# Gathering two expert rows per turn instead of four through a ring of eight places, with a quarter of the query weights kept in SBUF

## The chip, the cores and the metric

The kernel runs on one core of one Trainium2 chip. The metric is the device time of one launch in microseconds. The engines are TensorE (PE; its weight loads are listed apart as PEld), VectorE (DVE), ScalarE (ACT), GpSimd (POOL) and SyncE (SP); SP and POOL issue the transfers, which 16 DMA engines carry out.

## The reference

Two layers over 256 tokens of width 1024, everything in float32. Each layer has a mixer (four groups of heads, one output projection) and then an expert retrieval, which is where most of the bytes are:

```python
def peer(h, wq, keys, u_tab, v_tab):
    ...
        q = (xc @ wq).reshape(c, PEER_HEADS, 2, PEER_QDIM // 2)        # wq: 1024 x 2048
        sc = jnp.einsum('thpd,hpkd->thpk', q, keys, ...)
        top_v, top_i = lax.top_k(sc, PEER_TOPK)                         # 16 of 128, twice a head
        cand = (top_v[:, :, 0, :, None] + top_v[:, :, 1, None, :]).reshape(c, PEER_HEADS, -1)
        ...
        best_v, best_pos = lax.top_k(cand, PEER_TOPK)
        ids = jnp.take_along_axis(cand_id, best_pos, axis=-1)
        gate = jax.nn.softmax(best_v, axis=-1)
        ug = u_tab[ids]                                                 # 8 x 16 rows of 1024 for each token
        act = jax.nn.gelu(jnp.einsum('td,thkd->thk', xc, ug, ...)) * gate
        vg = v_tab[ids]
        return jnp.einsum('thk,thkd->td', act.astype(vg.dtype), vg)
```

Each token has 128 experts (8 heads, 16 each) of its own, and each expert is a row of u and a row of v, 4 KB each.

## The kernel before

The 256 tokens are two blocks of 128, one token to a partition. A pass n (0 to 3) is one block of one layer: passes 0 and 1 are layer 0, passes 2 and 3 are layer 1. In a pass, a slot is one of the 128 experts of all 128 tokens of the block. One indirect transfer of POOL (L1817) gathers u and v rows of one slot, 1 MB, into a place of `ring`, which has `RING` = 10 places. 512 slots go through it in all.

A turn takes `RING_G` = 4 slots. DVE makes the dot product of each u row with the block's normalised tokens as soon as the place has landed (L1354, "dots"). When the turn's four dots are there, ACT applies gelu (L839) and DVE multiplies by the gates (L1363, "weigh"). ACT then writes a diagonal matrix for each slot (L862), and PE adds diag x v to the PSUM sums in banks 0 and 1 (L1756, "rows of v"): four MATMUL records for each slot. When PE is through with a slot, `v_used` rises, and POOL gathers the next slot into that place. In turns 20 to 30 of passes 0 to 2, DVE adds the v row of the turn's fourth slot itself (L1370). The last two turns of all go slot by slot (L1377, L1384, L852, L1767).

The mixer and the expert search of the next pass are computed between turns. `plan_steps` writes one list of steps, and each engine walks it in order and does its part of each step; no scheduler changes it. In the turns 0 to 25 of a pass, the steps of the next pass stand between "weigh" and "rows of v": in turn 18 the transposes of its normalised rows ("rows 1", L1430), in turns 19 to 23 its query products ("query 0" to "query 3", L1720, each 1024 x 512 weights), scores (L1740) and searches ("best", "pairs", "ids", all on DVE).

Query weights are four quarters of 2 MB per layer (`wq_quarters`, `wq_at`). Quarter 0 stays in W for both passes of a layer. Quarters 1 to 3 are loaded by SP in each pass: in pass 0 partly into ring places that are not in use yet (quarter 1 into places 8 and 9, quarter 2 into 0 and 1), in pass 2 in 12 pieces of 512 KB, in passes 1 and 3 as L630, L631 and, when query 1 is through, L633. The first gathers wait for those ring places: gathers 6 and 7 for query 1 and gathers 8 and 9 for query 2 (`t in (6, 8)`).

## Time and profile before

| | |
|---|---|
| three runs, median (lowest to highest) | 1575.87 us (1573.58 to 1576.57) |
| the profiled execution, its time | 1571.93 us |
| its span, first to last instruction | 1570.1 us |
| PE, DVE, ACT, POOL busy | 1353.3, 1155.8, 454.2, 607.5 us |
| bytes moved | 627.87 MB, 400 GB/s on average |
| mean granted clock of TensorE | 0.957 |

The profiled execution lies 1.83 us above its span and 3.94 us below the median of the three runs. A windows view gives, for each stretch, the busy time of each engine, then the granted clock of PE, the mean share of the 16 DMA engines that were busy (1.01 is full) and the rate. "Idle before" is the time an engine stood still just before a group or an instruction, with what ended it.

### The profile page before, as it was taken

What the parts mean: (1) busy time and instruction counts of PE and PEld (TensorE: products, weight loads), DVE (VectorE), ACT (ScalarE), POOL (GpSimd) and SP (SyncE); (2) the same over time, 40 slices, a digit from 0 to 9 for tenths busy, and PEclk for the clock granted to TensorE, in tenths of its full rate; (3) what the DMA queues carried; (4) which work ended last, traced back from release to release, by engine and by line L of the source; (5) the groups of instructions that cost most, each with busy time, mean ns of one, the idle gap of its engine ahead of it and who ended that gap; (6) DMA issues with size and microseconds to landing.
All of it is one profiled execution on the core that took longest, in us unless ns stands there. A gap on an engine that the chain in (4) does not pass through costs nothing.

```text
span 1570.1 us, 15089 instructions
## 1 busy us (share of the span) xinstructions
PE 1353.3 (86%) x4622; PEld 735.0 (47%) x4622; DVE 1155.8 (74%) x2745; ACT 454.2 (29%) x1095; POOL 607.5 (39%) x525
## 2 busy tenths in 40 slices
PE   8899999998795997888897799999869777878777
PEld 4667455553472444453375345555337433333333
DVE  6937999787697886874578888985658987665545
ACT  3523154352211333342122134333212221121112
POOL 1012455444333334453433333644433443333331
PEclk9999999999898998999999899999979999999999
DMA  9558999999999999999999999999999999999997
GB/s 359 220 207 350 421 419 422 398 421 421 420 394 421 422 407 418 421 419 423 421 418 418 418 410 413 418 380 401 422 423 392 415 411 420 423 421 421 422 421 326
DMA packets 89820, 627.87 MB, mean 400 GB/s; under 512 B 10081, under 2 KB 11361, under 8 KB 20750
## 3 DMA queue, kind: packets, MB, share of 16 engines
q0 software_dynamic: 74144, 537.97, 83.2%
q1 hardware_dynamic: 15598, 88.95, 14.0%
q8 instruction: 38, 0.62, 0.2%
q14 instruction: 40, 0.33, 0.1%
HBM read 625.82 MB, written 1.06 MB: 399 GB/s over the span
## 4 chain that ended last, share of the span: by engine, by line
PE 41%; DMA 33%; DVE 16%; issue 6%; ACT 3%; POOL 1%; SPq 0%; POOLq 0%; DVEq 0%; ACTq 0%
DMA ring<-table_uv,ids 31%; PE ps L1756 24%; DVE ring L1354 6%; PE ps L1720 5%; PE ps L1520 4%; PE ps L1687 2%; PE ps L1510 1%; DMA ring<-w_in 1%; ACT acts L839 1%; ACT diag L862 1%; PE ps L1471 1%; PE ps L1587 1%; DVE weights L1363 1%; PE ps L1493 1%; POOL ring L1817 1%
## 5 line engine op out<-in xcount | busy, mean ns | idle before, releaser
L1756 PE MATMUL ps<-ring,diag 128*128 128x512 f32 x1884 | 877.3, 620 | 193.2 <-ACT diag L862 186.1
L1817 POOL DMA_INDIRECT ring<-table_uv,ids x512 | 601.9, 1175 | 927.0 <-PE ps L1756 780.1
L1756 PEld LDWEIGHTS ps<-ring,diag 128*128 128x128 f32 x1884 | 365.8, 199 | 654.6 <-issue 643.9
L1354 DVE CUSTOM_DVE_ANT_0 ring<-ring,h 128x1024 f32<-128x1024 f32 x384 | 456.3, 1224 | 155.5 <-DMA ring<-table_uv,ids 152.8
L839 ACT ACTIVATE acts<-dots,small 128x4 f32<-128x4 f32 x126 | 37.5, 297 | 875.5 <-DVE dots L1354 849.6
L1354 DVE CUSTOM_DVE_ANT_0 ring<-ring,ps 128x1024 f32<-128x1024 f32 x120 | 144.7, 1220 | 98.1 <-DMA ring<-table_uv,ids 97.9
L862 ACT ACTIVATE diag<-cst,weights 128x128 f32<-128x128 f32 x471 | 151.3, 390 | 28.9 <-DVE weights L1363 28.9
L1720 PEld LDWEIGHTS ps<-hT,W 128*128 128x128 f32 x896 | 101.9, 192 | 3.7 <-issue 2.9
L1720 PE MATMUL ps<-hT,W 128*128 128x128 f32 x896 | 103.1, 276 | 0.2 <-ACT hT L708 0.2
L1520 PE MATMUL ps<-W,hT 128*128 128x512 f32 (+2 forms) x160 | 60.1, 530 | 1.3 <-DVE hT L985 1.3
L1363 DVE TENSOR_TENSOR weights<-acts,gates 128x4 f32<-128x4 f32 x126 | 20.5, 163 | 51.4 <-ACT acts L839 51.4
L1687 PE MATMUL ps<-W,hT 128*128 128x512 f32 x128 | 57.3, 593 | 0.8 <-DVE hT L1199 0.8
L839 ACT ACT_TABLE_LOAD x43 | 55.2, 1283 | 2.2 <-DVE dots L1354 1.5
L1520 PEld LDWEIGHTS ps<-W,hT 128*128 128x128 f32 x160 | 30.4, 190 | 33.0 <-issue 30.6
L1370 DVE SCALAR_TENSOR_TENSOR x<-ring,weights,x 128x1024 f32<-128x1024 f32 x33 | 42.4, 1285 | 1.2
L1354 DVE DVE_READ_ACCUMULATOR2_ANT dots<- 128x1 f32 x504 | 41.4, 82 | 0.0
L1687 PEld LDWEIGHTS ps<-W,hT 128*128 128x128 f32 x128 | 24.0, 190 | 29.2 <-issue 28.2
L1510 PE MATMUL ps<-W,hT 128*128 128x512 f32 (+2 forms) x96 | 35.3, 523 | 1.3 <-DVE hT L985 1.3
L1587 PE MATMUL ps<-W 128*128 128x256 f32 (+1 forms) x128 | 32.0, 332 | 3.6 <-DVE h L1166 2.3
L770 ACT ACTIVATE W<-ps,small 128x128 f32<-128x128 f32 (+1 forms) x64 | 26.0, 418 | 12.3 <-DVE small L1135 12.2
L1134 DVE TENSOR_REDUCE small<-ps 128x4 f32<-128x512 f32 (+1 forms) x16 | 15.2, 953 | 17.7 <-PE ps L1594 10.2
L1510 PEld LDWEIGHTS ps<-W,hT 128*128 128x128 f32 x96 | 18.2, 190 | 19.4 <-issue 17.2
(319 smaller groups left out, 1201.1 us busy)
## 6 DMA issues: line engine op xcount, KB each, us to landing
W<-peer_wq SPq DMA_DIRECT2D x9, 2048.0 KB, 12.8
W<-w_out SPq DMA_DIRECT2D x6, 2048.0 KB, 12.5
W<-w_in SPq DMA_DIRECT2D x8, 1282.0 KB, 11.3
ring<-table_uv,ids POOLq DMA_INDIRECT x512, 13.4
W<-w_in SPq DMA_DIRECT2D x8, 898.0 KB, 10.0
W<-peer_wq SPq DMA_DIRECT2D x12, 512.0 KB, 13.1
W<-w_in SPq DMA_DIRECT2D x8, 768.0 KB, 9.8
W<-w_in SPq DMA_DIRECT2D x8, 514.0 KB, 11.8
```

The costliest lines, as they stand in the source:

```text
L839: a.activation(acts[:, g * RING_G:(g + 1) * RING_G], dots[:, g * RING_G:(g + 1) * RING_G], ACT.Gelu_apprx_tanh, scale=ffn_rstd[n % NB]).th ...
L862: a.activation(diag[:, s, :], ident, ACT.Copy, scale=weights[:, s:s + 1]).then_inc(diag_ready, 1)
L1354: v.tensor_tensor_reduce(ring_u[:, r, :], ring_u[:, r, :], tokens, 1.0, 0.0, ALU.mult, ALU.add, dots[:, s:s + 1]).then_inc(dots_done, 1)
L1363: v.tensor_tensor(weights[:, ss], acts[:, ss], gates[:, b, i * RING_G:(i + 1) * RING_G], ALU.mult)\
L1370: v.scalar_tensor_tensor(out=x[:, b, :], in0=ring_v[:, r, :], scalar=weights[:, s:s + 1], in1=x[:, b, :], op0=ALU.mult, op1=ALU.add).then_ ...
L1510: mm = pe.matmul(ps[:, 2 + i, 0:c1 - c0], hT[:, k, :], win_at(n)[:, k % 2, c0:c1], start=(k == 0), stop=(k == KC - 1))
L1520: mm = pe.matmul(ps[:, z_bank(n, i), 0:c1 - c0], hT[:, k, :], win_at(n)[:, slot, c0:c1], start=(k == 0), stop=(k == KC - 1))
L1587: pe.matmul(dst, q, k, start=True, stop=False)
L1687: mm = pe.matmul(ps[:, 2 + c, :], hT[:, k, :], half[:, k % 4, c * 512:(c + 1) * 512], start=(k == 0), stop=(k == KC - 1))
L1720: mm = pe.matmul(ps[:, 6 + q % 2, i * P:(i + 1) * P], src[:, k, :], hT[:, k, :], start=(k == 0), stop=(k == KC - 1))
L1756: mm = pe.matmul(ps[:, c, :], diag[:, s, :], ring_v[:, r, c * 512:(c + 1) * 512], start=(k == 0), stop=(k == SLOTS - 1), skip_group_check= ...
L1817: gp.indirect_dma_start(ring[:, place(t), :], None, table_uv, bass.IndirectOffsetOnAxis(ap=ids[:, b, k:k + 1], axis=0)).then_inc(pair_in[p ...
```

## The change

It does five things.

- A turn has two slots (`RING_G` = 2), so a pass has 64 turns instead of 32. The buffers for dots, weights and diagonals still hold 8 slots, which are now four turns (`BACK` = 4) instead of two.
- The ring has 8 places. In the room of the two others stands `wq_kept`: quarter 2 of the query weights is loaded once a layer and stays for its second pass. Passes 1 and 3 load quarters 1 and 3 only, both at once; pass 2 loads them in 8 pieces, and quarter 2 earlier. In pass 0, quarter 1 lies in places 0 and 1 (gathers 6 and 7 wait for query 1), and gather 8 onward waits for the release of gather 0 onward.
- The steps between turns: the list of each old turn is cut in the middle, first half in the first of its two new turns. A list of one step, and all of turn 0, goes to the second. In pass 0 the first searches are placed by a table (`first_search`), and ACT's copies of query 2 and 3 by steps of their own ("queried").
- The last slot of all: DVE adds its v row to the PSUM sums by two SCALAR_TENSOR_TENSOR of 512 columns (L1408 after the change) in place of diagonal, product and sum. The tokens x are added to PSUM by PE half way through pass 3.
- Behind two exponentials in pass 0, ACT does a small gelu, so that its table is loaded early.

```diff
-RING_G = 4
-HELD = 2 * RING_G
-RING = 10
-PLACES = (7, 2, 3, 4, 5, 6, 8, 9, 0, 1)
+RING_G = 2
+HELD = 8
+BACK = HELD // RING_G
+RING = 8
+PLACES = (7, 2, 3, 4, 5, 6, 0, 1)
+QUAD = 4 // RING_G
+TURNS = HALVES // QUAD
-SINGLE = HALVES * PASSES - 2
+SINGLE = HALVES * PASSES - HELD // RING_G
...
+    first_search = {2: ["best 1"], 4: ["best 2"], 5: ["best 3"], 6: ["pairs 1"], 7: ["ids 1"], 9: ["pairs 2"], 11: ["ids 2"]}
...
+            turn, part = i // QUAD, i % QUAD
+            turn_steps = [(name, n) for name in (own[turn] if n and turn < len(own) else [])]
+            turn_steps += [(name, n + 1) for name in (mixing[turn] if turn < len(mixing) else [])]
...
+            cut = len(turn_steps) // 2 if turn else 0
+            turn_steps = turn_steps[cut:] if part else turn_steps[:cut]
...
+        wq_kept = sb("wq_kept", [P, 4096])
...
-        wq_early = [by_key(t) for t in (pool[:, 16384:20480], pool[:, 0:4096], W[:, 2560:6656])]
+        wq_early = [by_key(t) for t in (pool[:, 0:4096], W[:, 2560:6656])]
...
-                sp.dma_start(wq_at(n, 1), wq_quarters[1]).then_inc(wq_in[1], 16)
-                sp.dma_start(wq_at(n, 2), wq_quarters[2]).then_inc(wq_in[0], 16)
-                sp.wait_ge(qT_ps, 4 * n + 2)
+                sp.dma_start(wq_at(n, 1), wq_quarters[1]).then_inc(wq_in[0], 16)
                 sp.dma_start(wq_at(n, 3), wq_quarters[3]).then_inc(wq_in[1], 16)
...
-                    v.wait_ge(low_done, 1)
-                    v.tensor_tensor(x[:, b, 0:512], x[:, b, 0:512], ps[:, 0, :], ALU.add).then_inc(x_low, 1)
-                    v.wait_ge(v_used, by_pe(HALVES * (n + 1)))
-                    v.tensor_tensor(x[:, b, 512:D], x[:, b, 512:D], ps[:, 1, :], ALU.add).then_inc(x_done, 1)
+                    v.wait_ge(weights_done, parts_done(m - 1) + k % RING_G + 1)
+                    v.wait_ge(v_used, by_pe(HALVES * (n + 1)) - 1)
+                    for c, done in ((0, x_low), (1, x_done)):
+                        v.scalar_tensor_tensor(out=x[:, b, c * 512:(c + 1) * 512], in0=ring_v[:, r, c * 512:(c + 1) * 512],
+                                               scalar=weights[:, sl:sl + 1], in1=ps[:, c, :], op0=ALU.mult, op1=ALU.add).then_inc(done, 1)
...
-                        elif t in (6, 8):
-                            gp.wait_ge(qT_ps, t // 2 - 1)
+                        elif t == 6:
+                            gp.wait_ge(qT_ps, 2)
```

PE's order at the first gathers of pass 0, before. L1720 is a query product, L1740 scores, L1756 rows of v, L1430 the transposes for pass 1, L1520 the projection of pass 1 (the input weights are W).

```order
L1740 MATMUL ps<-key_rows,zkv 128x128 x4
L1720 MATMUL ps<-hT,ring 128x128 x32
L1756 MATMUL ps<-ring,diag 128x512 x8
L1740 MATMUL ps<-key_rows,h 128x128 x4
L1720 MATMUL ps<-hT,W 128x128 x32
L1740 MATMUL ps<-key_rows,zkv 128x128 x4
L1430 MATMUL ps<-cst,x 128x128 x8
L1756 MATMUL ps<-ring,diag 128x512 x8
L1520 MATMUL ps<-W,hT 128x512 x3
```

The same place after the change (L1734 query, L1754 scores, L1770 rows of v, L1447 transposes, L1537 projection):

```order
L1754 MATMUL ps<-key_rows,zkv 128x128 x4
L1734 MATMUL ps<-hT,wq_kept 128x128 x32
L1770 MATMUL ps<-ring,diag 128x512 x8
L1754 MATMUL ps<-key_rows,h 128x128 x4
L1734 MATMUL ps<-hT,W 128x128 x32
L1770 MATMUL ps<-ring,diag 128x512 x4
L1447 MATMUL ps<-cst,x 128x128 x8
L1770 MATMUL ps<-ring,diag 128x512 x4
L1754 MATMUL ps<-key_rows,zkv 128x128 x4
L1770 MATMUL ps<-ring,diag 128x512 x4
L1537 MATMUL ps<-W,hT 128x512 x3
```

Query 2 reads `wq_kept` instead of the ring. The first four slots still follow it; the next four (two new turns) follow query 3 directly, and the scores of query 3 stand behind them.

DVE's order at the same place, before. L1354 is a dot product (two instructions a slot), L1363 the weights, L1286 the start of "pairs".

```order
L1354 ISA ring,dots<-ring,h 128x1024
L1354 ISA dots 128x1
L1354 ISA ring,dots<-ring,h 128x1024
L1354 ISA dots 128x1
L1354 ISA ring,dots<-ring,h 128x1024
L1354 ISA dots 128x1
L1354 ISA ring,dots<-ring,h 128x1024
L1354 ISA dots 128x1
L1363 TENSOR_TENSOR weights<-acts,gates 128x4
L1286 TENSOR_TENSOR W<-W 128x256
```

After the change (L1368 dots, L1377 weights, L1300 pairs):

```order
L1368 ISA ring,dots<-ring,h 128x1024
L1368 ISA dots 128x1
L1368 ISA ring,dots<-ring,h 128x1024
L1368 ISA dots 128x1
L1377 TENSOR_TENSOR weights<-acts,gates 128x2
L1368 ISA ring,dots<-ring,h 128x1024
L1368 ISA dots 128x1
L1368 ISA ring,dots<-ring,h 128x1024
L1368 ISA dots 128x1
L1377 TENSOR_TENSOR weights<-acts,gates 128x2
L1300 TENSOR_TENSOR W<-W 128x256
```

DVE writes weights, and so stands for ACT's gelu, behind two dots instead of behind four.

PE's order from the transposes of pass 1 ("rows 1", L1430, then L1435) to its second query product, before:

```order
L1430 MATMUL ps<-cst,x 128x128 x8
L1435 MATMUL ps<-W,cst 128x512 x2
L1756 MATMUL ps<-ring,diag 128x512 x6
L1720 MATMUL ps<-hT,W 128x128 x32
L1756 MATMUL ps<-ring,diag 128x512 x6
L1740 MATMUL ps<-key_rows,W 128x128 x4
L1720 MATMUL ps<-hT,W 128x128 x32
```

After the change:

```order
L1447 MATMUL ps<-cst,x 128x128 x8
L1452 MATMUL ps<-W,cst 128x512 x2
L1770 MATMUL ps<-ring,diag 128x512 x6
L1734 MATMUL ps<-hT,W 128x128 x32
L1770 MATMUL ps<-ring,diag 128x512 x6
L1754 MATMUL ps<-key_rows,W 128x128 x4
L1770 MATMUL ps<-ring,diag 128x512 x4
L1734 MATMUL ps<-hT,W 128x128 x32
```

The six products behind L1452 are two turns now, 4 + 2, each released by its own weights. The first half of the turn with query 1 goes ahead of that query.

## Rows read from the trace of the kernel before

**Rows 1.** The page: DMA share and rate in 40 slices of the span.

```profile
DMA  9558999999999999999999999999999999999997
GB/s 359 220 207 350 421 419 422 398 421 421 420 394 421 422 407 418 421 419 423 421 418 418 418 410 413 418 380 401 422 423 392 415 411 420 423 421 421 422 421 326
```

**Rows 2.** The page: DMA issues, KB each, median us from issue to landing.

```profile
ring<-table_uv,ids POOLq DMA_INDIRECT x512, 13.4
...
W<-peer_wq SPq DMA_DIRECT2D x12, 512.0 KB, 13.1
```

**Rows 3.** Five windows of 5 us with the least DMA: first, worst, last.

```profile
300.00:305.00 5.00, 5.00 (x19) 2.61 (x18) 5.00 (x8) 0.27 (x1) 4.39 (x3) 1.00 0.90 336
...
1055.00:1060.00 5.00, 5.00 (x12) 2.27 (x11) 5.00 (x9) 0.13 (x1) 3.95 (x3) 0.88 0.77 295
1210.00:1215.00 5.00, 5.00 (x19) 2.74 (x18) 4.53 (x12) 1.28 (x4) 4.26 (x3) 1.00 0.87 342
```

**Rows 4.** Windows: the first gathers, and four stretches of queries and search.

```profile
126.00:142.00 16.00, 15.31 (x92) 11.30 (x91) 12.40 (x51) 5.64 (x10) 7.01 (x7) 1.00 0.73 268
...
142.00:240.00 98.00, 95.56 (x327) 51.81 (x326) 88.69 (x240) 31.88 (x71) 45.01 (x32) 1.00 1.01 419
420.00:480.00 60.00, 56.44 (x329) 41.53 (x329) 52.45 (x148) 15.11 (x33) 24.73 (x21) 0.99 0.99 402
1174.00:1234.00 60.00, 58.51 (x350) 43.74 (x348) 51.90 (x148) 14.46 (x30) 24.93 (x23) 1.00 0.99 402
1240.00:1280.00 40.00, 29.05 (x63) 12.32 (x62) 37.67 (x113) 10.10 (x24) 17.90 (x16) 0.95 1.00 404
```

**Rows 5.** Waits of DVE for gathers, 142 to 240 us (total, times, longest).

```profile
DVE ring L1354 <- DMA ring<-table_uv,ids: 0.7, 1, 0.7
```

**Rows 6.** Timelines of PE and POOL, first gathers (start, duration, idle before).

```profile
127.96 7.31 PE L1720 MATMUL ps<-hT,ring 128*128 128x128 f32 x64
...
142.87 7.31 PE L1720 MATMUL ps<-hT,W 128*128 128x128 f32 x64
...
136.05 0.94 POOL L1817 DMA_INDIRECT ring<-table_uv,ids  x1 [6.86 <-PE ps L1720]
...
155.42 0.94 POOL L1817 DMA_INDIRECT ring<-table_uv,ids  x1 [12.07 <-PE ps L1756]
```

**Rows 7.** Timelines of PE, DVE, POOL and SP's queue around 400 us.

```profile
410.27 7.48 PE L1756 MATMUL ps<-ring,diag 128*128 128x512 f32 x12 [11.55 <-ACT diag L862]
...
400.54 1.23 DVE L1354 CUSTOM_DVE_ANT_0 ring<-ring,h 128x1024 f32<-128x1024 f32 x1 [0.77 <-DMA ring<-table_uv,ids]
407.93 1.23 DVE L1354 CUSTOM_DVE_ANT_0 ring<-ring,h 128x1024 f32<-128x1024 f32 x1 [6.15 <-DMA ring<-table_uv,ids]
...
414.29 1.66 POOL L1817 DMA_INDIRECT ring<-table_uv,ids  x1 [14.86 <-PE ps L1756]
...
438.12 0.33 SPq L633 DMA_DIRECT2D W<-peer_wq  x1
```

**Rows 8.** The page: groups (busy, mean ns, idle before).

```profile
L839 ACT ACTIVATE acts<-dots,small 128x4 f32<-128x4 f32 x126 | 37.5, 297 | 875.5 <-DVE dots L1354 849.6
L1363 DVE TENSOR_TENSOR weights<-acts,gates 128x4 f32<-128x4 f32 x126 | 20.5, 163 | 51.4 <-ACT acts L839 51.4
```

**Rows 9.** Chain that ended last, its last pieces (start, us).

```profile
1563.83 0.09 DVE dots L1377
...
1563.95 0.30 ACT acts L846
...
1564.27 0.17 DVE weights L1384
...
1564.47 0.41 ACT diag L852
...
1565.01 1.97 PE ps L1767 x4
...
1567.01 0.69 DVE x L1392
```

More of the change, by code:

```diff
@@ L205, in plan_steps @@
         if n == 0:
-            own = [[name for name in names if name.split()[0] in ("best", "pairs", "ids")] for names in inner]
-            mixing = [[name for name in names if name.split()[0] not in ("best", "pairs", "ids")] for names in inner] + middle + search
+            own, mixing = [], inner + middle + search
         else:
@@ L219, in plan_steps @@
             plan.append(("dots", n, i))
+            if n == 0 and i in (0, 2):
+                do(["query 2" if i == 0 else "query 3"], n)
             plan.append(("weigh", n, i))
@@ L222, in plan_steps @@
                 plan.append(("gathered", n - 1, 0))
[L223 to L225 removed]
+            if n == 0 and i == 1:
+                do(["pairs 5", "ids 5", "queried 2"], n)
+            if turn == 0:
                 plan.append(("rows of v", n, i))
[L227 to L234 removed]
+            if n == 0 and i == 1:
+                do(["score 2"], n)
+            if n == 0 and i == 3:
+                do(["queried 3"], n)
             if n == 0:
[L236 to L239 removed]
+                do(first_search.get(i, []), n)
+            for name, m in turn_steps:
+                do([name], m)
+            if turn:
                 plan.append(("rows of v", n, i))
+            if n == 0 and i == 3:
+                do(["score 3"], n)
     plan.append(("gathered", PASSES - 1, 0))
@@ L808, in query, with queried @@
             def query(n, i):
+                if n or i not in (2, 3):
+                    queried(n, i)
+            def queried(n, i):
                 if i == 4:
@@ L825, in find_ids @@
                 a.activation(part, part, ACT.Exp, scale=ffn_rstd[n % NB]).then_inc(gate_exp, 1)
+                if n == 0 and i in (4, 5):
+                    a.activation(small[:, 410:411], cst[:, C_ID:C_ID + 1], ACT.Gelu_apprx_tanh)
             def h_out(n, i):
@@ L867, in _ @@
                   "weights": head_weights, "co sums": co_sums, "s5 out": s5_output, "gate rows": gate_rows, "glu": glu_out,
-                  "mixed rows": mixed_rows, "query": query, "ids": find_ids, "h out": h_out, "dots": take_dots, "weigh": weigh, "dot": take_dot, "weigh one": weigh_one})
+                  "mixed rows": mixed_rows, "query": query, "queried": queried, "ids": find_ids, "h out": h_out, "dots": take_dots, "weigh": weigh, "dot": take_dot, "weigh one": weigh_one})
         @block.vector
@@ L1758, in add_rows @@
                     mm.then_inc(v_used, 1)
+                if (n, i) == (PASSES - 1, HALVES // 2):
+                    for c in range(2):
+                        pe.matmul(ps[:, c, :], ident, x[:, n % NB, c * 512:(c + 1) * 512], start=False, stop=False, skip_group_check=True)
             def add_row(n, k):
+                if k == SLOTS - 1:
+                    return
                 t, s = SLOTS * n + k, k % HELD
```

117 lines of the change are left out of this document (50 added, 67 removed).

## The prediction

> **What bounds the kernel now.** I read the strip of DMA first [rows 1]. The reader is to see two halves: four slices with gaps, then 36 in which the DMA engines are full, at 421 GB/s where only gathers run. One gather is 1.05 MB, so one place takes 2.49 us, and no engine that is faster can change that. From 145 us on the time is bytes over 421 GB/s, plus the moments in which the queue runs dry, plus what comes behind the last gather. The moments are few: the five worst windows of 5 us after 150 us lack 0.10, 0.13, 0.19, 0.23 and 0.13 of their DMA share, together 3.9 us [rows 3]. In all five PE is busy for the whole window and DVE for 90% or more of it, so there the consumers are late, not the transfers. The windows of longer stretches say which consumer: PE is 95.56 us busy of 98, 56.44 of 60, 58.51 of 60, and only from 1240 to 1280 it is DVE (37.67 of 40, PE 29.05) [rows 4]. Before that, from 142 to 240 us, DVE waited for a gather once, for 0.7 us [rows 5]. So the kernel is bound by DMA, with PE just under it around queries and projections, and DVE just under it in the searches.
>
> **Bytes.** Two loads of a quarter go (pass 1 and pass 3), 2 x 2.097 MB. At 421 GB/s that is 2 x 4.98 = 9.96 us. The loads of pass 2 are only moved. The Trainium skill, "DMA: Bandwidth & Descriptors", section "Anatomy of one DMA", gives a transfer a fixed 2.0 us beside bytes over 436 GB/s. By it a quarter would cost an estimated 6.8 us and the two 13.6. I leave the fixed part out, since a 512 KB piece needs 13.1 us to land [rows 2] while its bytes are 1.2 us: it stands in a full queue, and what goes from that queue is bytes. The term is -10.0 us, if the queue stays full where the loads were. That is not certain. The third quarter of a pass (L633) was loaded from 438.1 [rows 7], inside the full stretch of PE from 420 to 480 [rows 4], and by the same wait for query 1 inside that from 1174 to 1234; no load stands there any more. If PE's work there neither shrinks nor starts earlier, the queue only runs dry earlier and the term is 0.
>
> **Does PE start earlier?** Around 400 us a turn of four shows its price. Three slots had landed and DVE had taken the third by 401.8, then DVE stood 6.15 us for the fourth. PE stood 11.55 us for the first diagonal, and POOL 14.86 us for a place [rows 7]. With two slots to a turn, weights, diagonals and rows of v of the first two follow at about 401, some 9 us earlier. PE has that much less left when its full stretch begins, so I take the bytes as gained. The same pattern stands ahead of the queries of passes 2 and 3.
>
> **The ring.** In the even stretches a turn of four is held like this: the last slot lands; the dot takes 1.3 us, then gelu, weights, diagonal and their gaps 1.2 us [rows 9], then 1.7 us of PE to a slot. The four places come free 4.1, 5.9, 7.6 and 9.3 us after that landing, and the first landed 7.5 us before it, which makes 10.5 us on average, or 4.2 places of 10. With two, it is 4.1 and 5.9 us with a wait of 2.5 or 0 ahead, 6.3 us, or 2.5 places of 8. In flight are 5.8 before and 5.5 after. The median of 13.4 us from issue to landing [rows 2] is 5.4 places, so the count is right, and the smaller ring costs nothing there: 0. Where the consumers are late, shorter holds should help and two missing places hurt. The bounds are the 3.9 us of the five windows gone, or as much again. Since four of the five lie at steps that the cut divides, I take half of them away: -2.0 us.
>
> **The start.** Gathers 8 and 9 went out from 136.05, as soon as query 2 had left the ring, and 10 to 13 behind them, since slots 0 to 3 came free meanwhile [rows 6]. From 126 to 142 the DMA share was 0.73 [rows 4]. Now gather 8 needs slot 0's rows of v, which start when query 2 ends (127.96 + 7.31 = 135.3 [rows 6]) and take 1.7 us: it goes out at 137.1, one us later. Twelve are out by 142, and gather 12 must wait for rows of v behind query 3, which ends at 150.2: it goes out at about 152. Before, gathers 12 and 13 were out by 142.4, and gather 14 went at 155.4 [rows 6]. Gathers 8 to 11 are 4 x 2.49 = 10 us of DMA from about 139 to 149, and SP's next loads, released by query 3, bring bytes from about 152. The queue is empty 2.5 us there and 1 us earlier: +3.5 us (0 if the dry spot is filled, 7 if pass 0 stays late).
>
> **The doubled small steps.** 126 turns of four become 252 of two: 126 more gelus on ACT (0.297 us each, 37 us) and 126 more products on DVE (0.163 us) [rows 8]. ACT is busy 454 us of 1570 and hides its part behind its own waits for dots (849.6 us). DVE's part is more than the product: it stands 0.41 us for ACT each time (51.4 / 126) and pays 0.16 less some overlap, 0.53 us for each old turn. 126 x 0.53 = 67 us is the upper bound, 0 the lower. Where DVE waits for gathers, it is hidden by that wait. From 142 to 240, 420 to 480 and 1174 to 1234 it is hidden by PE [rows 4]. Without that cover it would cost 10 turns x 0.53 = 5.3 us in the first stretch and 3.2 in each other. Only from 1240 to 1280 DVE alone is full: 4 turns x 0.53 = +2.1 us. The other steps between turns, ACT's table loads among them, stay as many. The rule that speaks against the change is in the Trainium skill, "Perfetto Trace Analysis", section "Optimizing Scalar/DVE Operations": larger operations are better on a saturated engine, and breaking up pays where an engine isn't saturated but makes others wait. By its first half, with DVE taken as saturated in all four stretches, the term would be 13.8 us; it is a rival below.
>
> **The tail.** From the end of the last dot (1563.92) to the end of the last sum (1567.70) the chain is gelu 0.30, weights 0.17, diagonal 0.41, four matmuls 1.97, sum 0.69, with gaps [rows 9]. The last three go, and two SCALAR_TENSOR_TENSOR of 512 columns come, one behind the other. The trace has none of that shape; the sum of 512 columns takes 0.69, so 2 x 0.69 from about 1564.6 to 1566.0: -1.7 us (between -2.4, if only one were on the path, and 0, if PE's backlog holds slot 126 back).
>
> **Sum.** -10.0 - 2.0 + 3.5 + 2.1 - 1.7 = -8.1 us. Against the profiled execution that is 1563.8 of 1571.93; that execution lies 3.9 us under the median of the runs, and against the median it is 1567.8. 0.2% (3.2 us) is about what a measurement of this kernel can tell from no change.
>
> **The rivals.**
> - *DVE becomes the limit* (slower). Mechanism: the second stop for gelu in each old turn. It decides once DVE's lateness exceeds PE's in the four stretches. For it: DVE is 88.69 of 98, 52.45 of 60, 51.90 of 60 and 37.67 of 40 busy there [rows 4], and one wait for a gather in 98 us [rows 5]. Against it: PE is fuller in three of them. Price: 26 turns x 0.53 = 13.8 us instead of 2.1, and the two removed loads gain nothing, as DMA was no limit there; without the -2.0 of the ring too: 13.8 + 3.5 - 1.7 = +15.6 for the full case, and about +6 if half of it holds. That is 1582 (up to 1591).
> - *The bytes are gained only half, or the start costs double* (no change). PE's full stretches keep their ends: -10.0 becomes -3 to -5, the start +3.5 to +7. Sum -1 to 0: 1575.
> - *More is gained.* Short holds remove all dry moments (-3.9), PE's earlier start covers DVE in the search too (0), and the start's dry spot is filled by SP's loads (0): -10.0 - 3.9 - 1.7 = -15.6, 1560.
>
> **How the numbers follow.** The forecast has 0.47 (-4 to -12), the larger gain 0.21, no change 0.13, slower 0.19. The range leaves out a tenth at each end: 1558 to 1580. Faster by over 0.2% is forecast plus larger gain, 0.68; within 0.2% 0.13; slower 0.19.
>
> **What would show it.** Bytes 623.7 MB instead of 627.9. POOL's long stops of 12 us and more gone around 400 and 1160 us, and PE's waits for diagonals there about half. Windows from 126 to 155 us with a share of DMA 3 us poorer. 252 weights with about 0.4 us of wait each, and no lower rate than 421 GB/s in the last 250 us. The span's end 4.5 us behind the last dot instead of 6.2 (1570.1 - 1563.92). I am wrong if the plateau has more than 10 us of missing DMA share: then the smaller ring or DVE has eaten the bytes.

## The result and the profile after

| | before | after |
|---|---|---|
| median (lowest to highest) | 1576.19 us (1573.58 to 1576.57, 4 runs) | 1605.66 us (1598.74 to 1607.27, 4 runs) |
| span of the profiled execution | 1570.1 us | 1605.5 us |
| bytes moved | 627.87 MB | 623.72 MB |

The changed kernel is slower: ratio 1.0187, 95% interval 1.0165 to 1.0209. The prediction was 1567.8 us with a range from 1558 to 1580; the time lies outside, on the other side of before. The granted clock is not the reason: 0.947 to 0.956 in the four runs after, 0.944 to 0.954 in ten runs of before beside two_ring10.

The page of the changed kernel: the strips of PE, DVE and DMA, and the sum of the bytes.

```profile
PE   8899999999796898989888699999889787788777
...
DVE  6827899787698877874669886976658986764555
...
DMA  9448999999999999999999999999999999999998
GB/s 359 208 157 317 421 395 421 373 393 423 420 366 422 380 421 387 421 394 416 422 419 404 406 365 416 422 389 375 422 423 372 359 390 421 420 410 423 421 421 345
DMA packets 89106, 623.72 MB, mean 388 GB/s; under 512 B 10001, under 2 KB 11281, under 8 KB 20158
```

The bytes went as predicted. But where the rate stood at 421 with few dips [rows 1], every third slice or so now has a dip to between 359 and 395. PE is busy for 86% of the span and DVE for 73%, as before (86 and 74). The time is missing in the queue, all over the plateau (from 160 us on). Windows show how much. First before (stretch, busy time of PE, PEld, DVE, ACT and POOL, then granted clock, share of DMA, rate), then after:

```profile
110.00:160.00 50.00, 47.77 (x307) 37.87 (x306) 40.85 (x162) 13.14 (x26) 15.94 (x17) 1.00 0.89 347
160.00:400.00 240.00, 225.88 (x711) 119.19 (x709) 208.33 (x461) 90.97 (x205) 120.22 (x90) 1.00 1.01 417
400.00:800.00 400.00, 336.76 (x1189) 185.18 (x1190) 294.65 (x686) 112.27 (x278) 161.17 (x132) 0.94 1.01 417
800.00:1200.00 400.00, 358.12 (x1273) 201.45 (x1272) 300.99 (x706) 118.48 (x280) 164.96 (x134) 0.94 1.00 411
1200.00:1555.00 355.00, 278.58 (x704) 125.92 (x703) 235.98 (x542) 69.09 (x190) 139.30 (x141) 0.95 1.01 418
```

```profile
110.00:160.00 50.00, 47.99 (x322) 39.38 (x321) 36.71 (x142) 17.00 (x35) 12.45 (x13) 1.00 0.77 298
160.00:400.00 240.00, 225.44 (x707) 118.89 (x707) 206.60 (x488) 98.22 (x226) 99.52 (x87) 0.99 0.99 404
400.00:800.00 400.00, 341.02 (x1126) 181.49 (x1125) 295.97 (x726) 124.25 (x303) 146.56 (x132) 0.93 0.99 405
800.00:1200.00 400.00, 360.98 (x1268) 201.18 (x1266) 299.11 (x701) 128.34 (x308) 150.76 (x134) 0.96 0.99 404
1200.00:1590.00 390.00, 304.00 (x805) 138.80 (x806) 264.11 (x639) 90.86 (x242) 142.88 (x148) 0.94 0.99 406
```

Against 421 GB/s, a stretch lacks its length times (1 - rate / 421). For the four long rows that is 2.3, 3.8, 9.5 and 2.5 us before, 18 in all, and 9.7, 15.2, 16.1 and 13.9 us after, 55: +37. The row from 110 to 160 gives 8.8 and 14.6: +6. Ahead of 110 us it is +4 more (260 and 243 GB/s), the last 15 us give back 2, and the removed bytes 10. 37 + 6 + 4 - 2 - 10 = 35, and the span grew by 35.4. This sum closes by itself, since a span is its bytes over 421 plus what is missing. What it tells is where the missing time lies: 37 us of it on the plateau, where the prediction had set the ring at nothing. What put it there, only the experiments can say. Of the 10 us ahead of 160 us, some 7 go with the first gather, which came at 116.99 us instead of 109.74 (see the last section). The profiled execution after is also the slowest of its four, and that of before is faster than all four of before; the medians differ by 29.5 us.

One of the worst moments shows how it comes. Windows of the changed kernel, then PE, DVE and POOL around 600 us (start, duration, idle before):

```profile
535.00:540.00 5.00, 5.00 (x11) 2.14 (x10) 4.76 (x10) 2.94 (x5) 1.70 (x2) 0.82 0.74 280
600.00:605.00 5.00, 5.00 (x15) 2.47 (x15) 4.57 (x12) 2.50 (x7) 1.38 (x2) 1.00 0.55 203
925.00:930.00 5.00, 5.00 (x12) 2.20 (x11) 4.76 (x12) 2.08 (x3) 2.59 (x2) 0.91 0.49 162
```

```profile
592.08 8.77 PE L1537 MATMUL ps<-W,hT 128*128 128x512 f32 x24
...
592.52 0.94 POOL L1834 DMA_INDIRECT ring<-table_uv,ids  x1 [0.78 <-PE ps L1770]
...
594.15 0.16 DVE L1377 TENSOR_TENSOR weights<-acts,gates 128x2 f32<-128x2 f32 x1 [0.36 <-ACT acts L851]
...
597.52 0.75 DVE L1050 TENSOR_SCALAR h<-ps,small 128x512 f32<-128x512 f32 x1 [3.20 <-PE ps L1537]
...
599.60 0.48 DVE L1050 TENSOR_SCALAR h<-ps,small 128x256 f32<-128x256 f32 x1 [1.33 <-PE ps L1537]
...
602.84 0.94 POOL L1834 DMA_INDIRECT ring<-table_uv,ids  x1 [9.39 <-PE ps L1770]
```

PE does two projections in a row, 8.77 us. Meanwhile no place comes free, and POOL stands 9.39 us. DVE has only the two dots of this turn, then its own step, which stands for PE (3.20 and 1.33 us). The windows around 535 and 925 us have the same shape: PE busy throughout, DMA at 0.74 and 0.49.

The groups of the doubled steps, the gathers' issue to landing, and the end of the chain of waits, after:

```profile
L851 ACT ACTIVATE acts<-dots,small 128x2 f32<-128x2 f32 x252 | 74.4, 295 | 815.8 <-DVE dots L1368 795.5
...
L1377 DVE TENSOR_TENSOR weights<-acts,gates 128x2 f32<-128x2 f32 x252 | 40.9, 162 | 112.6 <-ACT acts L851 112.6
...
ring<-table_uv,ids POOLq DMA_INDIRECT x512, 11.5
```

```profile
1599.52 1.97 PE ps L1786 x4
...
1601.60 0.75 DVE x L1408
1602.34 0.66 DVEq L256
```

DVE's stop for gelu comes twice as often, 0.45 us each. A gather lands 11.5 us after its issue instead of 13.4 [rows 2], which at 2.49 us each is 4.6 places in flight instead of 5.4.

One thing the text ahead of the prediction says wrongly: the steps of the next pass stand in turns 0 to 31, not 0 to 25 ("rows 1" in turn 24, "query 0" in 25, the search in 26 to 31). No number rests on it.

### The profile page after: what moved, and what is told of

Same layout as the page of the kernel before. It is cut to its first block, busy times and chain, and to the rows that moved or that the text cites. A ratio compares the mean times of both kernels' runs of the same rounds, so it can differ in the third digit from the quotient of the medians.

```text
span 1605.5 us, 15831 instructions
## 1 busy us (share of the span) xinstructions
PE 1383.9 (86%) x4622; PEld 743.8 (46%) x4622; DVE 1175.7 (73%) x2871; ACT 505.6 (31%) x1222; POOL 557.5 (35%) x525
## 2 busy tenths in 40 slices
DMA packets 89106, 623.72 MB, mean 388 GB/s; under 512 B 10001, under 2 KB 11281, under 8 KB 20158
## 4 chain that ended last, share of the span: by engine, by line
PE 44%; DMA 24%; DVE 18%; issue 9%; ACT 3%; POOL 1%; SPq 0%; DVEq 0%; ACTq 0%; POOLq 0%
PE ps L1770 25%; DMA ring<-table_uv,ids 23%; DVE ring L1368 5%; PE ps L1734 5%; PE ps L1537 3%; PE ps L1527 2%; PE ps L1704 2%; ACT acts L851 2%; POOL ring L1834 1%; DMA ring<-w_in 1%; PE ps L1488 1%; ACT diag L876 1%; DVE weights L1377 1%; DVE x L1384 1%; PE ps L1651 1%
## 5 line engine op out<-in xcount | busy, mean ns | idle before, releaser
L1770 PE MATMUL ps<-ring,diag 128*128 128x512 f32 x1884 | 903.6, 630 | 197.5 <-ACT diag L876 187.4
L1834 POOL DMA_INDIRECT ring<-table_uv,ids x512 | 552.2, 1078 | 1015.3 <-PE ps L1770 872.2
L1770 PEld LDWEIGHTS ps<-ring,diag 128*128 128x128 f32 x1884 | 366.6, 201 | 664.6 <-issue 650.7
L1368 DVE CUSTOM_DVE_ANT_0 ring<-ring,h 128x1024 f32<-128x1024 f32 x384 | 459.1, 1223 | 103.0 <-DMA ring<-table_uv,ids 96.9
L851 ACT ACTIVATE acts<-dots,small 128x2 f32<-128x2 f32 x252 | 74.4, 295 | 815.8 <-DVE dots L1368 795.5
L1368 DVE CUSTOM_DVE_ANT_0 ring<-ring,ps 128x1024 f32<-128x1024 f32 x120 | 145.4, 1221 | 87.3 <-DMA ring<-table_uv,ids 87.1
L876 ACT ACTIVATE diag<-cst,weights 128x128 f32<-128x128 f32 x471 | 165.1, 394 | 57.9 <-DVE weights L1377 57.9
L1377 DVE TENSOR_TENSOR weights<-acts,gates 128x2 f32<-128x2 f32 x252 | 40.9, 162 | 112.6 <-ACT acts L851 112.6
L1734 PEld LDWEIGHTS ps<-hT,W 128*128 128x128 f32 x704 | 81.7, 194 | 5.3 <-issue 4.7
L1734 PE MATMUL ps<-hT,W 128*128 128x128 f32 x704 | 82.0, 277 | 0.2 <-ACT hT L714 0.2
L1537 PE MATMUL ps<-W,hT 128*128 128x512 f32 (+2 forms) x160 | 60.5, 529 | 0.0
L1537 PEld LDWEIGHTS ps<-W,hT 128*128 128x128 f32 x160 | 30.4, 190 | 33.2 <-issue 32.5
L1368 DVE DVE_READ_ACCUMULATOR2_ANT dots<- 128x1 f32 x504 | 41.7, 83 | 0.0
L1704 PEld LDWEIGHTS ps<-W,hT 128*128 128x128 f32 x128 | 25.0, 198 | 31.8 <-issue 30.7
L1734 PEld LDWEIGHTS ps<-hT,wq_kept 128*128 128x128 f32 x256 | 29.1, 192 | 1.4 <-issue 1.4
L1734 PE MATMUL ps<-hT,wq_kept 128*128 128x128 f32 x256 | 29.2, 275 | 0.0
## 6 DMA issues: line engine op xcount, KB each, us to landing
ring<-table_uv,ids POOLq DMA_INDIRECT x512, 11.5
```

The costliest lines, as they stand in the source:

```text
L851: a.activation(acts[:, g * RING_G:(g + 1) * RING_G], dots[:, g * RING_G:(g + 1) * RING_G], ACT.Gelu_apprx_tanh, scale=ffn_rstd[n % NB]).th ...
L876: a.activation(diag[:, s, :], ident, ACT.Copy, scale=weights[:, s:s + 1]).then_inc(diag_ready, 1)
L1368: v.tensor_tensor_reduce(ring_u[:, r, :], ring_u[:, r, :], tokens, 1.0, 0.0, ALU.mult, ALU.add, dots[:, s:s + 1]).then_inc(dots_done, 1)
L1377: v.tensor_tensor(weights[:, ss], acts[:, ss], gates[:, b, i * RING_G:(i + 1) * RING_G], ALU.mult)\
L1537: mm = pe.matmul(ps[:, z_bank(n, i), 0:c1 - c0], hT[:, k, :], win_at(n)[:, slot, c0:c1], start=(k == 0), stop=(k == KC - 1))
L1704: mm = pe.matmul(ps[:, 2 + c, :], hT[:, k, :], half[:, k % 4, c * 512:(c + 1) * 512], start=(k == 0), stop=(k == KC - 1))
```

## The experiments

Names give the slots to a turn and the places of the ring. The kernel before was run beside each group; its medians were 1573.2 to 1575.7 us, so the ratios are what is compared across groups. "Missing" is what the share of DMA lacks to 1.00, summed over windows of 5 us from 160 us to 15 us before the end, of the profiled execution. It shows only about half of what the rate shows (19 us more after than before, where the rate gives 37), so it serves to compare kernels and is no account of their time.

| kernel | median us | ratio to before, interval | missing us |
|---|---|---|---|
| before | 1576.19 | 1 | 7.3 |
| after | 1605.66 | 1.0187, 1.0165 to 1.0209 | 26.0 |
| two_ring10 | 1585.24 | 1.0064, 1.0043 to 1.0084 | 12.8 |
| two_ring9 | 1596.70 | 1.0135, 1.0110 to 1.0159 | 15.9 |
| two_ring8_reload | 1607.06 | 1.0197, 1.0170 to 1.0225 | 22.2 |
| four_ring8 | 1643.42 | 1.0423, 1.0393 to 1.0453 | 47.3 |
| four_ring10_reload | 1584.89 | 1.0064, 1.0044 to 1.0084 | 6.9 |
| four_ring10_tail | 1575.29 | 1.0000, 0.9990 to 1.0009 | 5.2 |
| four_ring10_stop | 1597.70 | 1.0137, 1.0119 to 1.0155 | 18.2 |
| four_ring10_spare | 1577.96 | 1.0019, 1.0002 to 1.0036 | 7.9 |
| four_ring10_split | 1574.56 | 1.0011, 0.9993 to 1.0029 | 8.2 |
| four_ring10_lag | 1575.42 | 1.0012, 0.9994 to 1.0030 | 4.7 |
| two_ring10_lag | 1585.34 | 1.0071, 1.0048 to 1.0095 | 11.5 |
| two_ring10_uncut | 1709.51 | 1.0847, 1.0830 to 1.0865 | 95.2 |
| two_ring10_first | 1680.34 | 1.0679, 1.0649 to 1.0709 | 78.0 |
| two_ring10_first_ahead | 1620.37 | 1.0300, 1.0251 to 1.0349 | 35.1 |
| two_ring10_ahead | 1582.46 | 1.0061, 1.0040 to 1.0082 | 12.2 |
| two_ring8_even | 1600.98 | 1.0169, 1.0149 to 1.0190 | 22.6 |
| two_ring10_even | 1579.17 | 1.0038, 1.0016 to 1.0060 | 9.5 |
| two_ring10_even_ahead | 1580.07 | 1.0045, 1.0023 to 1.0067 | 10.8 |

### Places and bytes

two_ring10 is the changed kernel with ten places, and so with quarter 2 loaded in every pass again.

```diff
-RING = 8
-PLACES = (7, 2, 3, 4, 5, 6, 0, 1)
+RING = 10
+PLACES = (7, 2, 3, 4, 5, 6, 8, 9, 0, 1)
...
-        wq_kept = sb("wq_kept", [P, 4096])
...
```

> The changed kernel with a ring of ten places again, and without the kept quarter (quarter 2 is loaded in every pass as before); turns of two, the order of the steps and the last slot stay changed. Theory A, the two missing places are what costs (the steps between turns are too long for eight places): 1572 to 1580 us, within 0.4% of before. Theory B, DVE's doubled stops for gelu and the new order cost: 1595 to 1610 us, as slow as the changed kernel or slower, since 10 us of bytes come back.

four_ring8 is the kernel before with eight places and the kept quarter.

```diff
-RING = 10
-PLACES = (7, 2, 3, 4, 5, 6, 8, 9, 0, 1)
+RING = 8
+PLACES = (7, 2, 3, 4, 5, 6, 0, 1)
...
+        wq_kept = sb("wq_kept", [P, 4096])
...
```

> The kernel before with the ring of eight and the kept quarter alone; turns of four, their steps and the last slot as before. Theory A: 1605 to 1635 us, slower than the changed kernel, since a turn of four holds more of the eight places. Theory B: 1565 to 1575 us, the bytes are gained and nothing is lost.

two_ring8_reload is the changed kernel with quarter 2 loaded once more in passes 1 and 3, to the same place.

```diff
                 sp.dma_start(wq_at(n, 1), wq_quarters[1]).then_inc(wq_in[0], 16)
+                sp.dma_start(wq_at(n, 2), wq_quarters[2]).then_inc(wq_kept_in, 16)
+                sp.wait_ge(qT_ps, 4 * n + 2)
                 sp.dma_start(wq_at(n, 3), wq_quarters[3]).then_inc(wq_in[1], 16)
...
```

> The changed kernel, but quarter 2 is loaded again in passes 1 and 3, into the same kept room; so it moves as many bytes as before. If the two removed loads are worth their bytes in the changed kernel: 10 us slower than it, about 1616. If the queue runs dry there anyway: as the changed kernel, 1603 to 1608.

two_ring9 is two_ring10 with the gathers using nine places.

```diff
-RING = 10
-PLACES = (7, 2, 3, 4, 5, 6, 8, 9, 0, 1)
+RING = 9
+PLACES = (7, 2, 3, 4, 5, 6, 8, 0, 1)
...
```

> As the run with turns of two and ten places, but POOL uses nine of the ten. Theory A: between the ring of ten and the ring of eight with as many bytes, 1585 to 1600 us; the second missing place costs more than the first. Theory B: the same as with ten places, within 3 us.

four_ring10_reload is the kernel before with quarter 2 loaded twice in passes 1 and 3.

```diff
                 sp.dma_start(wq_at(n, 1), wq_quarters[1]).then_inc(wq_in[1], 16)
+                sp.dma_start(wq_at(n, 2), wq_quarters[2]).then_inc(wq_again, 16)
+                sp.wait_ge(wq_again, 16 * (n // NB + 1))
                 sp.dma_start(wq_at(n, 2), wq_quarters[2]).then_inc(wq_in[0], 16)
```

> Before, with quarter 2 loaded twice in passes 1 and 3, the second time when the first has landed: 4.2 MB more, 10 us at 421 GB/s. Theory A (bytes are time while the queue is full, and the prediction's 10 us were lost only since the changed kernel's queue runs dry there): 1580 to 1586. Theory B (the consumers set the time around these loads in the kernel before too): at most 1577.

Measured with turns of two at the same bytes: ten places 1585.24, nine 1596.70, eight (reload) 1607.06. A place is worth 11.5 us and then 10.4. So the two missing places are the larger part of the loss; two_ring10 itself lies between its two theories, 9.7 us over before. The expectation for nine places held, but not its "second missing place costs more than the first". With the two loads back at eight places the time rises by 1.4 us of 10: that cannot be told from nothing, and it is less than 10 clear of the noise. In the kernel before the same 4.19 MB cost 0.64%, 10.1 us (by the interval 6.9 to 13.2), and by bytes over 421 GB/s it is 10.0. So the price of bytes was about right. Two windows of four_ring10_reload, over the loads, show a full queue, where the kernel before has 407 and 408 GB/s there:

```profile
400.00:480.00 80.00, 65.10 (x351) 45.84 (x350) 58.58 (x158) 15.81 (x38) 25.26 (x22) 0.89 1.01 422
1150.00:1240.00 90.00, 75.83 (x382) 50.76 (x381) 62.18 (x160) 17.98 (x44) 30.44 (x28) 0.92 1.01 422
```

By these rates the kernel before lacked 5.4 us in the two stretches, and the extra bytes could have gone there for nothing; why they cost their full price all the same is not shown.

The Trainium skill, "DMA: Bandwidth & Descriptors", section "Anatomy of one DMA — SWDGE (gpsimd) path", gives a transfer issued by GpSimd a fixed 2.0 us beside its bytes. Carried over to these loads, which SP issues, it would give an estimated 13.6 us for the two. The measured 10.1 lies nearer to the bytes alone, and 13.6 just outside the interval.

four_ring8 shows the other side: at eight places turns of four are far worse (1.0423, 8 us beyond its theory A) than turns of two (1.0187), by 37 us. At ten places turns of two cost 10.

Where PE has no steps, the reason can be read. These are the 250 us that end 15 us before the span does, in which PE adds rows of v (in the first two kernels the tokens x too) and nothing else, in two_ring10, after and four_ring8:

```profile
1320.70:1570.70 250.00, 193.21 (x412) 78.03 (x411) 145.16 (x295) 56.08 (x159) 92.00 (x98) 0.96 1.01 421
1340.50:1590.50 250.00, 193.63 (x412) 78.04 (x411) 145.32 (x295) 56.11 (x159) 94.43 (x100) 0.96 1.01 419
1386.10:1636.10 250.00, 192.47 (x380) 79.72 (x381) 132.29 (x257) 44.77 (x129) 87.84 (x93) 0.88 0.98 389
```

The kernel before and two_ring9 have 421 there too. With turns of two, eight places cost about 1 us of these 250; with turns of four, 19. So turns of two do need fewer places, and what two missing places cost them lies where PE has steps. From two_ring10 to two_ring8_reload the missing time by the rate grows by 20.7 us on the plateau. 7 of them lie in windows of 5 us with a DMA share below 0.90 (9 windows, then 14), the other 13.5 in windows that lack less. The example at 600 us is thus one of the worst moments, and most of the price is a little missing at many steps.

### The stop for gelu

four_ring10_stop is the kernel before with one more gelu of two dots and one more small product of DVE behind the second dot of each turn, into a spare buffer.

```diff
+                a.wait_ge(dots_done, RING_G * m + 2)
+                a.activation(spare[:, 0:2], dots[:, g * RING_G:g * RING_G + 2], ACT.Gelu_apprx_tanh,
+                             scale=ffn_rstd[n % NB]).then_inc(spare_gelu, 1)
...
+                    if j == 1:
+                        v.wait_ge(spare_gelu, m + 1)
...
+                        v.tensor_tensor(spare[:, 2:4], spare[:, 0:2], gates[:, b, i * RING_G:i * RING_G + 2], ALU.mult)
```

> The kernel before (turns of four, ring of ten) with one more stop: behind the second dot of each turn, ACT does a gelu of the two dots into a spare tile, DVE waits for it and multiplies two columns; nothing else uses the result. It doubles DVE's stops and changes nothing else. If the doubled stops are what makes turns of two slower at a ring of ten: 7 to 12 us above before, about 1585. If they are hidden as the prediction had it: 0 to 3 us above it.

four_ring10_spare has the same instructions, with DVE's wait and product behind the third dot.

```diff
-                    if j == 1:
+                    if j == 2:
```

> The run with the added gelu and product in each turn of four (1597.7), with one thing moved: DVE's wait for that gelu and its small product stand behind the third dot instead of behind the second, by when the gelu is long done. Same instructions, no stop. Theory A (the stop of 0.41 us costs, each instruction of 0.16 us hardly): 1574 to 1582. Theory B (added work costs wherever it stands; in the split run it was only made good by places that came free earlier): 1590 to 1600.

Waits of DVE from 150 to 1545 us (total, times, longest), first of the run with the stop, then of the one with it moved:

```profile
DVE ring L1361 <- DMA ring<-table_uv,ids: 172.8, 144, 6.2
DVE spare L1367 <- ACT spare L841: 70.9, 120, 6.5
DVE weights L1376 <- ACT acts L846: 44.1, 121, 0.4
```

```profile
DVE ring L1361 <- DMA ring<-table_uv,ids: 231.5, 177, 6.1
DVE weights L1376 <- ACT acts L846: 45.2, 124, 0.4
...
DVE spare L1367 <- ACT spare L841: 10.9, 6, 5.4
```

The stop costs: 1597.70 with it, 1577.96 without, for the same work (by the ratios 18.6 us). The run with the stop lies above both of its expectations; for the moved stop theory A held. The added gelu and product cost 0.19%, 3 us. What the reader should see is the first row. In before, DVE waits 250.6 us for gathers in this stretch. 71 us of stops come and 78 us of these waits go, as if the stops only filled idle time, and yet the time rises by 22 us. So a wait of DVE for a gather was not room in which a stop costs nothing.

four_ring10_split does in earnest what turns of two want of this: gelu, weights and diagonals of the first two slots apart, the weights behind the third dot.

```diff
+                    if j == 2:
+                        weigh_part(n, i, 0)
...
```

> Before, with gelu, weights and diagonals in two parts: the first two slots' weights are written behind the third dot, so that DVE does not stand for that gelu, and those places come free earlier. It has the doubled small instructions of turns of two but not the doubled stop. Theory A (the stop of 0.41 us costs, not the instruction of 0.16 us): 1572 to 1582, that is at least 15 us under the run with the doubled stop (1597.7). Theory B (any added piece on DVE or ACT costs): 1590 to 1600.

four_ring10_lag and two_ring10_lag write a turn's weights behind the first dot of the next turn, where no other step of DVE stands between.

```diff
+                    if j == 0 and held_back:
+                        weigh(*held_back.pop())
...
```

> Before, with a turn's weights behind the first dot of the next turn wherever no other step of DVE stands between: no stop of DVE for gelu in these turns, each place of a turn held up to 1.3 us longer. Theory A (DVE's stops cost time also in the kernel before, 0.41 us each): 1560 to 1572. Theory B (the stops of turns of four are hidden; only the held places count): 1576 to 1590.

> Turns of two, ring of ten, and DVE writes a turn's weights behind the first dot of the next turn wherever no other step of DVE stands between, so that it no longer stands for the gelu. Theory A (the doubled stop of DVE is what turns of two cost, 9.7 us at ten places): at most 1577, since fewer stops are left than with turns of four. Theory B (what costs is the smaller block of slots at the steps, or ACT): 1582 to 1592, the later weights hold each place 1.3 us longer.

The split costs nothing that can be told, and gains nothing: 1.0011, as its theory A had it. Later weights change nothing either: turns of four stay as they were (1.0012), and turns of two at ten places too (1.0071 against 1.0064). Theory A of both failed, but neither run is a strong test. In four_ring10_lag DVE's waits for gelu fall only from 50 to 42 us, and in two_ring10_lag from 115 to 87, where before has 50; and each lagged turn holds its places longer, which can cost what the stops give back. So fewer stops in this way gain nothing, and whether the stops make up the 10 us of turns of two stays open.

### Steps and the run of dots

two_ring10_uncut puts all steps of an old turn into its second new turn, two_ring10_first all into the first (two_ring10 cuts the list in the middle).

```diff
-            cut = len(turn_steps) // 2 if turn else 0
+            cut = 0
...
```

> Turns of two with a ring of ten, as two_ring10 (1585 us), but the steps of an old turn are not cut: all stand in its second new turn, as the kernel before has them; only DVE's stops for gelu are doubled, and rows of v of the first two slots go ahead of the steps. If the cut costs: 1576 to 1580 us. If the stops cost (0.53 us for each old turn, hidden in part): as two_ring10 or slower, 1585 to 1592.

```diff
-            cut = len(turn_steps) // 2 if turn else 0
+            cut = len(turn_steps) if turn else 0
...
```

> Turns of two, ring of ten, and all steps of an old turn between weights and rows of v of its FIRST new turn (in the run before, all in the second: 1709.5, 124 us more than with the cut in the middle). Theory A (PE must not stand for a diagonal with steps still ahead of it): with the steps in the first new turn PE meets no row of v of the same old turn before the steps, so it walks on as before the change; 1577 to 1592. Theory B (what costs is a long block of steps within one short turn, wherever it stands, since only two slots are taken between blocks): as bad as the second-half run, over 1650.

All steps in the second new turn measured 1709.51, 124 us more than with the cut in the middle and far beyond both expectations (1576 to 1592). All steps in the first measured 1680.34: theory B, a long block of steps in a short turn is what costs wherever it stands, held. Why the second turn is 29 us worse than the first was not tried.

two_ring10_first_ahead is two_ring10_first, and two_ring10_ahead is two_ring10, with DVE making the next turn's two dots ahead of its steps; PE and ACT stay as they are.

```diff
+                if name == "dots" and i and (n or i >= 12) and mine[back - 1][0] == "weigh" and back < at:
+                    mine.insert(back, mine.pop(at))
...
```

> As the run with all steps in the first new turn (1680.3), with one thing moved, on DVE alone: where steps stand between a turn's weights and the next turn's dots, DVE makes those two dots ahead of its steps, so that it has four dots between the last weights and its steps again, as with turns of four. Theory A (turns of two halve the run of dots under which PE catches up, so DVE's steps stand for PE's: DVE waits for PE in steps were 162 us there, 35 in before): back to 1580 to 1610, waits for PE at most 70 us. Theory B (it is the block of steps itself, or the two slots that PE has around it): stays over 1640.

> Turns of two, ring of ten, steps cut in the middle, and the same move: DVE makes the next turn's dots ahead of its steps. Theory A: DVE's waits for PE in steps fall from 58 us to about 35 and the 9.7 us of turns of two at ten places shrink to 4 or less, 1573 to 1579. Theory B (the 9.7 us are the doubled stops for gelu): 1582 to 1590.

Waits of DVE from 150 to 1545 us, first of two_ring10_first, then of two_ring10_first_ahead:

```profile
DVE ring L1370 <- DMA ring<-table_uv,ids: 81.5, 73, 6.1
DVE h L1182 <- PE ps L1653: 29.7, 6, 5.9
DVE h L1179 <- PE ps L1653: 27.3, 6, 6.1
DVE small L1150 <- PE ps L1616: 23.4, 6, 5.0
```

```profile
DVE ring L1370 <- DMA ring<-table_uv,ids: 152.1, 124, 5.6
...
DVE small L1150 <- PE ps L1623: 15.3, 3, 6.8
...
DVE h L1182 <- PE ps L1663: 9.0, 6, 3.1
```

Summed over all such rows of the same view, DVE's waits for PE (in steps, all lines but the dots and weights) are as follows. The stretch is the same for all, though the slower kernels end later.

| kernel | waits for PE, us | for gathers | for gelu |
|---|---|---|---|
| before | 35 | 251 | 50 |
| after | 49 | 170 | 108 |
| two_ring10 | 59 | 144 | 115 |
| two_ring10_ahead | 18 | 185 | 112 |
| two_ring10_first | 162 | 82 | 113 |
| two_ring10_first_ahead | 62 | 152 | 104 |
| two_ring10_uncut | 173 | 63 | 123 |

Between two_ring10_first and its partner only the order on DVE differs, and it is worth 60 us; DVE's waits for PE fall by 100. That much is shown. The reading is this: PE must add the rows of v of the turn before ahead of its steps, and for those it needs that turn's weights. With four dots between these weights and DVE's own steps, PE has some 5 us (4 x 1.22) for it; with two dots DVE is there too early and stands. All steps in the first new turn cost 97 us against the cut in the middle (1.0679 against 1.0064). The move takes 60 of them; the other 37 are not explained by it, and the expectation of at most 1610 was missed by 10. With the lists cut in the middle the same move brings the waits from 59 to 18 us, but not the time (1.0061 against 1.0064): theory A failed there, and the waits for PE are no longer what costs. That the time lies in the range of theory B does not show that theory's cause.

two_ring8_even and two_ring10_even divide the steps of some old turns by hand, so that no new turn has more than one long step.

```diff
+            if turn in (26, 27):
+                turn_steps.sort(key=lambda step: step[0].startswith("query"))
             cut = len(turn_steps) // 2 if turn else 0
+            if n + 1 < PASSES:
+                cut = {26: 2, 27: 2}.get(turn, {1: 3, 3: 2, 5: 3}.get(turn, cut) if n else cut)
```

> The changed kernel (ring of eight, kept quarter) with the steps divided so that the long PE steps stand alone: in passes 1 and 2 one projection step less in the second new turns of turns 1, 3 and 5, and from pass 0 on the searches best 0 and best 1 ahead of query 1 and 2 instead of behind them. If it is long undivided steps that eight places can't bridge: 5 to 15 us faster than the changed kernel, 1591 to 1601. If the loss is spread over all steps: within 4 us of it.

> Turns of two, ring of ten, and the steps of a turn divided more evenly, as in the run with ring eight, where this was worth 4.7 us. Theory A (blocks of steps that are too long for two slots cost at any ring): 1576 to 1581. Theory B (only the short ring makes them cost): 1583 to 1587.

> Turns of two, ring of ten, steps divided more evenly and the next turn's dots ahead of DVE's steps. Theory A (both moves act on the same thing, DVE and PE meeting at the steps with too little run-ahead, and there is something left for the second): 1573 to 1578. Theory B (what is left after the even division is the doubled stops): 1578 to 1583.

The even division measured 4.7 us less by the medians at eight places (3 by the ratios, within the 4 us of its second expectation) and 0.26%, 4 us, at ten. In both pairs the intervals overlap, so a gain is likely but not shown. With dots ahead as well nothing is added (1.0045). two_ring10_even is the best version with turns of two, and it doesn't beat the kernel before.

### The last slot

four_ring10_tail is the kernel before with the last slot's v row on DVE, as in the change.

```diff
-                    v.tensor_tensor(x[:, b, 0:512], x[:, b, 0:512], ps[:, 0, :], ALU.add).then_inc(x_low, 1)
...
+                        v.scalar_tensor_tensor(out=x[:, b, c * 512:(c + 1) * 512], in0=ring_v[:, r, c * 512:(c + 1) * 512],
+                                               scalar=weights[:, sl:sl + 1], in1=ps[:, c, :], op0=ALU.mult, op1=ALU.add).then_inc(done, 1)
...
```

> The kernel before with only the change to the last slot: DVE adds its v row to PSUM, x is added by PE in the middle of pass 3. Expected from the rows of before: 1.7 us less, 1574; and nothing else moves. If it is no gain: within 0.5 us of before.

In its trace the span ends 4.6 us behind the last dot's end instead of 6.2. In the time nothing can be told: 1.0000, 0.9990 to 1.0009, so the expected 1.7 us (0.11%) did not show.

## Why the prediction was wrong, by its own steps

- **The ring, "0 there" and -2.0 at the dry moments: the step that failed.** It measured +21.8 us for two places. The count of places was made for the even stretches, and there it nearly holds: in the last 250 us eight places cost about 1 us, and a gather lands in 12.8 us, 5.1 places in flight where 5.5 were predicted. The ring pays off at the steps. An estimate for the worst of them: eight places are 8 x 2.49 = 19.9 us of queue. A slot caught by a block of PE is held 6.3 + 8.8 = 15.1 us (the prediction's hold, and the block at 592 us), so 4.8 us are left for issue to landing; with ten places it is 9.8 us. In four_ring8's last 250 us a gather lands in 9.0 us (median), and there the queue is just no longer full (0.98, 389 GB/s). The price of a place is shown; that blocks of this kind make it is argued, and they can't be all of it, since 13.5 of the 20.7 us lie in slighter gaps. The prediction did write "two missing places hurt" where the consumers are late, but bounded that by the 3.9 us that the kernel before lacked. That was no bound: a ring of ten had hidden the rest, and rows of before can't show what a smaller ring would uncover. The prediction's own sign of being wrong came true: more than 10 us of missing share, here 26, and it named the ring beside it.
- **"The cut divides" the long steps.** It divides the list by number, not by length. Two projections, 8.77 us, stand in one new turn. Dividing them more evenly measured 3 to 5 us less, with intervals that overlap.
- **The bytes, -10.0.** Mis-sized: -1.4 at eight places, which can't be told from 0. The price was right (+10.1 in the kernel before); its condition, "if the queue stays full where the loads were", didn't hold.
- **The doubled small steps, +2.1.** Failed in its reason, "where DVE waits for gathers, it is hidden by that wait". A doubled stop at turns of four costs 22 us, of which some 19 hang on where the wait stands. At 126 stops that is 0.17 us each, between the prediction's bounds of 0 and 0.53. The lag that a stop brings to a dot is passed on to the place's release, and so to the next gather. That this is the way it goes is argued from the rows of waits; no run shows it by itself. What the doubled stop costs in turns of two, where places are held for less time, no run shows: all of the change but the two places and the bytes costs 10 us together.
- **PE starts earlier.** Right in place: POOL's long stop behind 400 us is 9.00 us (until 420.63) instead of 14.86 [rows 7], and around 1160 us its longest is 4.21 instead of 15.92. PE's waits for diagonals from 380 to 480 us sum to 10.6 us instead of 18.3, and its longest on the plateau is 5.6 instead of 11.6. It brought nothing to the end.
- **The start, +3.5.** Right in mechanism: four gathers behind query 2's rows of v, then a stop until 159.42, where the prediction's 152 plus the 7.2 us by which this execution's first gather came later make 159.2. In the 50 us from each first gather on, the rate is 344 GB/s before and 318 after, which is +3.1 us. The +6 of the row from 110 to 160 us contains the later first gather.
- **The tail, -1.7.** Right in the trace (4.6 us behind the last dot; -1.6), not measurable in the time.
- **The rivals.** "DVE becomes the limit" gave the sign and up to 1591, by another way: DVE's share did not rise. No rival had the ring as its mechanism; slower had 0.19.

Added up: turns of two at ten places, with the new order and the last slot, +9.7 (1585.24 - 1575.56), two places +21.8, bytes -1.4. That makes +30.1, and the change measured +29.5. The sum goes from run to run and must close; the 0.6 are the two medians of before. What it gives is the share of each part.

**What stays open:** the 10 us of turns of two at ten places. The even division takes about 4 of them, with intervals that overlap; somewhat fewer stops for gelu and fewer waits for PE, each alone, take none. Whether the stops of the remaining turns make up the rest was not tried in one kernel. Of two_ring10_first, 37 of its 97 us over two_ring10 are open.

## What to carry to other kernels

A buffer ring's size is set by the moments in which places come free late, not by the mean in flight. An estimate that would have warned here: add to the even hold the longest block on the engine that frees the places, and see what is left for a transfer to land (4.8 us with eight places, 9.8 with ten, where 9.0 hardly filled the queue). The dry moments seen with the present ring are no bound for a smaller one. A wait that seems hidden behind another wait can still cost: here moving a wait behind one more dot was worth some 19 us for the same work, likely because both lie on one loop (landing, dot, release, next gather). And when turns are made shorter, the run of independent work ahead of a step that needs another engine gets shorter with them.

## What the runs showed of the hardware

The time of the first gather varies between profiled executions, from 109.25 to 116.99 us. With it goes a stretch at the lower granted clock (1.2 GHz instead of 2.4) that begins between 74.7 and 76.6 us: 3.4 us long in the profile of before and 20.5 us in that of after, 17.1 us in four_ring10_tail, which has the start of the kernel before and its first gather at 115.83 instead of 109.74. The seven profiles with ten places and turns of four have their first gather at 113.4 us on average, the four with eight places at 114.6. So of the 7.2 us by which the changed kernel's first gather comes later in the two profiles, at most about one is an effect of the change.
